# A two-block token mixer on one core: first norm on token rows, kept differences, low-rank products among the gate units

## The reference

```
h  = x * rsqrt(mean(x*x over channels) + 1e-6) * a_norm
xx = shift_one_token(h) - h
xr, xw, xk, xv, xa, xg = (h + xx * mu[j] for j in 0..5)
g = xg @ w_in[3]                          # 2048 columns, gate
w_log uses tanh(xw @ w1) @ w2             # w1: 1024 x 64
a     uses (xa @ a1) @ a2                 # a1: 1024 x 64
r, k, v = xr @ w_in[0], xk @ w_in[1], xv @ w_in[2]
... 32-head recurrence over 512 tokens gives y ...
x = x + y @ w_out
```

## Time and profile before

| | |
|---|---|
| median of 3 runs | 2349.39 us (2346.32 to 2353.45) |
| the profiled execution | 2350.47 us, span 2348.7 us |
| PE busy | 2116.7 us (90%), 16706 instructions |
| DVE busy | 1412.9 us (60%) |
| ACT busy | 1005.9 us (43%) |
| POOL busy | 266.6 us (11%) |
| DMA | 217.50 MB, mean 93 GB/s |

### The profile page before, as it was taken

One profiled execution on the slowest core, in us unless ns is written; L12 is line 12 of the kernel. 1 busy time (PEld: TensorE's weight loads), 2 busy tenths in 40 slices (PEclk: granted clock), 3 DMA queues, 4 the chain that ended last, 5 costly groups with the idle time before them and its releaser, 6 DMA issues.

```text
span 2348.7 us, 43326 instructions
## 1 busy us (share of the span) xinstructions
PE 2116.7 (90%) x16706; PEld 1653.7 (70%) x16706; DVE 1412.9 (60%) x2214; ACT 1005.9 (43%) x1768; POOL 266.6 (11%) x233
## 2 busy tenths in 40 slices
PE   2799999988888886989999999887989998999998
PEld 1577777767777774868888888566756675787876
DVE  6777777776676663355544555589755556434345
ACT  3464555545666664132322323321577324323233
POOL 2102000000233223000000000098000000000000
PEclk6899999989999997999999999899999998999998
DMA  3244555572324311323333333122211131333332
GB/s 107 63 129 143 166 168 169 167 180 59 76 68 95 93 30 61 96 73 96 90 103 91 89 97 99 48 78 63 82 45 37 53 90 54 97 91 91 101 90 76
DMA packets 396700, 217.50 MB, mean 93 GB/s; under 512 B 86144, under 2 KB 375320, under 8 KB 396312
## 3 DMA queue, kind: packets, MB, share of 16 engines
q1 hardware_dynamic: 395936, 215.40, 31.6%
q10 hardware_dynamic: 632, 0.21, 0.0%
HBM read 181.94 MB, written 33.62 MB: 92 GB/s over the span
## 4 chain that ended last, share of the span: by engine, by line
PE 67%; DVE 17%; ACT 8%; issue 5%; DMA 1%; SPq 1%; POOL 0%; DVEq 0%; ACTq 0%
PE bank L1502 17%; PE bank L1504 16%; PE bank L1503 16%; PE bank L520 3%; DVE dconv L1915 3%; DVE w_lo L1656 3%; PE bank L497 1%; ACT w_hi L1266 1%; PE bank L528 1%; DVE tmp L1705 1%; PE bank L443 1%; PE bank L429 1%; PE bank L471 1%; PE bank L874 1%; PE bank L865 1%
## 5 line engine op out<-in xcount | busy, mean ns | idle before, releaser
L1502 PE MATMUL bank<-xl,w_hi 128*128 128x512 f32 (+1 forms) x1696 | 689.1, 406 | 58.2 <-DVE xl L1661 40.6
L1503 PE MATMUL bank<-xl,w_lo 128*128 128x512 f32 (+1 forms) x1696 | 667.4, 393 | 0.0
L1504 PE MATMUL bank<-xl,w_hi 128*128 128x512 f32 (+1 forms) x1696 | 666.8, 393 | 0.0
L1266 ACT ACTIVATE w_hi<-w_raw 128x1024 fp32r<-128x1024 f32 (+1 forms) x282 | 295.6, 1049 | 426.3 <-PE bank L1504 421.7
L1502 PEld LDWEIGHTS bank<-xl,w_hi 128*128 128x128 f32 (+1 forms) x1696 | 321.1, 189 | 170.6 <-issue 53.5
L1656 DVE TENSOR_TENSOR w_lo<-w_raw,w_hi 128x1024 fp32r<-128x1024 f32 (+1 forms) x282 | 347.1, 1231 | 123.1 <-ACT w_hi L1266 112.1
L1503 PEld LDWEIGHTS bank<-xl,w_lo 128*128 128x128 f32 (+1 forms) x1696 | 322.1, 190 | 70.3 <-issue 7.4
L1504 PEld LDWEIGHTS bank<-xl,w_hi 128*128 128x128 f32 (+1 forms) x1696 | 321.5, 190 | 69.8 <-issue 1.6
L1502 PE MATMUL bank<-xh,w_hi 128*128 128x512 f32 x480 | 197.9, 412 | 50.3 <-DVE w_lo L1656 45.3
L1503 PE MATMUL bank<-xh,w_lo 128*128 128x512 f32 x480 | 191.9, 400 | 0.0
L1504 PE MATMUL bank<-xh,w_hi 128*128 128x512 f32 x480 | 191.3, 399 | 0.0
(11 more groups left out here) (310 smaller groups left out, 3070.5 us busy)
## 6 DMA issues: line engine op xcount, KB each, us to landing
w_raw<-in_a_w_in SPq DMA_DIRECT2D x64, 512.0 KB, 3.9
w_raw<-in_b_w_in SPq DMA_DIRECT2D x64, 512.0 KB, 4.0
w_raw<-in_w_ffn_up SPq DMA_DIRECT2D x44, 512.0 KB, 3.7
w_raw<-in_w_in SPq DMA_DIRECT2D x36, 512.0 KB, 3.7
w_raw<-in_a_w_out SPq DMA_DIRECT2D x16, 512.0 KB, 3.6
w_raw<-in_b_w_out SPq DMA_DIRECT2D x16, 512.0 KB, 3.7
w_raw<-in_w_ffn_down SPq DMA_DIRECT2D x16, 512.0 KB, 3.6
d_g<-sq SPq DMA_DIRECT2D x16, 256.0 KB, 2.1
```

The source lines that it names most:

```text
L1266: A(w_hi[0:rows, slot, 0:nkb, 0:ncol], w_raw[0:rows, slot, 0:nkb, 0:ncol], ACT.Copy).then_inc(s_hi, 1)
L1502: mm(outp, wh, xlo, start=start, stop=False)
L1503: mm(outp, wl, xhi, start=False, stop=False)
L1504: return mm(outp, wh, xhi, start=False, stop=stop)
```

## The change

What it does, part by part:

- x is loaded as four row blocks (128 tokens each) into `x_raw`. ACT squares a block with a sum along the row (`accum_out`) and makes the reciprocal root as one number a token; DVE scales the block in place; PE turns it. The eight banks hold the turned tiles, and ACT writes `hT` from them, with `a_norm` as the scale of the copy. `xT`, the eight squares, their sums and the PE sum go.
- The token differences are kept in `xx` (8 tiles, in the place of `xT`): tile 0 by DVE, tiles 1 to 7 by POOL. `shift_difference` in the gate turns goes.
- Units 0 and 1 (low-rank) go; the first unit is gate unit 0. The low-rank first products are made from h and xx instead of xw and xa: `xw @ w1 = h @ w1 + xx @ (mu * w1)`. POOL scales w1 and a1 by mu; their copies are split once by ACT and DVE. In each of the first four gate turns ACT makes the high parts of two tiles of h and two of xx (`lora_input`), POOL the low parts, and PE adds 12 matmuls into bank 6 behind the odd unit (`first_lora`). The hidden layer's steps follow in turns 4 to 7, and its last step stands behind turn 7.
- Parameters: one group is loaded by ACT's queue at first, the other three by SP's behind the first panels; they are turned behind unit 0 and copied behind turn 0.
- The store of `xT` and its load go. x is loaded a second time as rows (`x_back`) behind the last loads of the recurrence, PE turns it in the last turn of the recurrence's loop (`x_back_turned`), DVE copies it to `xT2` before it splits Y.

The core of the diff:

```diff
-U_LORA1 = 0
-U_GATE = U_LORA1 + 2
+U_GATE = 0
...
+            def x_back_turned(k):
+                if k == 0:
+                    pe.wait_ge(s_back, 16)
+                if k >= 4:
+                    pe.wait_ge(s_xt, k - 3)
+                for q in range(NT):
+                    last = tr(bank[k % 4][:, q * P:(q + 1) * P], x_back[:, q, k * P:(k + 1) * P], ident[:])
+                last.then_inc(s_xtr, 1)
...
+                    if t == PAIRS + 1 and s < DK:
+                        x_back_turned(s)
...
+            sp.dma_start(x_back[:], i["x"].rearrange("b (q p) d -> p (b q) d", p=P)).then_inc(s_back, 16)
             sp.wait_ge(R["y_finished"], CI)
-            sp.dma_start(xT2[:], d_x).then_inc(s_back, 16)
...
-            sp.wait_ge(s_xt, DK)
-            sp.dma_start(d_x, xT[:]).then_inc(s_spill, 16)
-            for u in range(4):
-                gate(u // 2, u % 2)
+            for q in range(NT):
+                sp.dma_start(x_raw[:, q, :], i["x"][0, q * P:(q + 1) * P, :]).then_inc(s_xin[q], 16)
+            gate(0, 0)
+            for n, mat in enumerate((i["a_w1"][0], i["a_a1"][0])):
+                sp.dma_start(w1_raw[:, 0, :, n * LORA:(n + 1) * LORA],
+                             mat.rearrange("(k p) c -> p k c", p=P)).then_inc(s_w1, 16)
+            gate(0, 1)
+            load_params(sp, range(1, 4), s_par[1])
+            for u in range(2):
+                gate(1, u)
...
+            for n, mu in enumerate((1, 4)):
+                gt.tensor_tensor(w1_raw[:, 1, :, cols], w1_raw[:, 0, :, cols], scale, ALU.mult).then_inc(s_w1m, 1)
+            for k in range(1, DK):
+                gp.wait_ge(s_hT, k + 1)
+                gt.tensor_tensor(xx[:, k, :], hT[:, k, 0:T], hT[:, k, 1:T + 1], ALU.subtract).then_inc(s_xx, 1)
+            for t in range(LORA_TURNS):
+                for n in range(4):
+                    gp.wait_ge(s_inhi, 4 * t + n + 1)
+                    gt.tensor_tensor(l_lo[:, n // 2, n % 2, :], ..., l_hi[...], ALU.subtract).then_inc(s_inlo, 1)
...
+            for q in range(NT):
+                act.wait_ge(s_xin[q], 16)
+                A(sq[:]..., x_raw[:, q, :], ACT.Square, accum_out=row_sum[:, q:q + 1]).then_inc(s_sq, 2)
+                act.wait_ge(s_sq, 2 * (q + 1))
+                o(A(r, row_sum[:, q:q + 1], ACT.Ln, bias=eps[:, 0:1], scale=1.0 / D))
+                A(r, r, ACT.Exp, scale=-0.5).then_inc(s_rs, 1)
+            w_high(0, 0, panels_by(0))
...
+            for k in range(DK + 2):
+                if k < DK:
+                    act.wait_ge(s_tr, k + 1)
+                    A(hT[:, k, 1:T + 1], bank[k][:], ACT.Copy, scale=col("a_norm", k)).then_inc(s_hT, 1)
+                if k >= 2:
+                    x_high(X_G + k - 2, xh[:, 0, k - 2, :], k % 2)
+                if k == DK - 1:
+                    act.wait_ge(s_w1, 32)
+                    first_weights(0)
+            first_weights(1)
...
+            for t in range(LORA_TURNS):
+                gate(t)
+                if t + 1 < LORA_TURNS:
+                    lora_input(t + 1)
+            act.wait_ge(s_lora, LORA_TURNS)
+            gate(LORA_TURNS)
+            act.wait_ge(s_lmax, 1)
+            z = acc[rows2[0], :]
+            o(A(z, z, ACT.Exp, scale=-2.0))
+            o(A(z, z, ACT.Ln, bias=1.0))
+            A(z, z, ACT.Exp, scale=-1.0).then_inc(s_lsig, 1)
...
+            def first_lora(t):
+                pe.wait_ge(s_inlo, 4 * (t + 1))
+                for n in range(4):
+                    last = three(bank[6][:], w1_hi[:, n % 2, 2 * t + n // 2, :], w1_lo[...], l_hi[...], l_lo[...], ...)
+                last.then_inc(s_lora, 1)
...
+            for q in range(NT):
+                dve.wait_ge(s_rs, q + 1)
+                V.tensor_scalar(x_raw[:, q, :], x_raw[:, q, :], row_rstd[:, q:q + 1], None, ALU.mult).then_inc(s_sqa, 2)
+            w_low(0, 0)
...
-                    if u == 0:
-                        shift_difference(t)
...
+            dve.wait_ge(s_lhi, 1)
+            V.tensor_tensor(lora[:, 1, :], acc[:], lora[:, 0, :].bitcast(F32), ALU.subtract).then_inc(s_lt, 1)
...
+            dve.wait_ge(R["y_summed"], CI)
+            for k in range(DK):
+                dve.wait_ge(s_xtr, k + 1)
+                if k == DK - 2:
+                    dve.wait_ge(R["y_finished"], CI - 1)
+                V.tensor_copy(xT2[:, k, :], bank[k % 4][:]).then_inc(s_xt, 1)
```

More of the change, by code:

```diff
@@ L1005, in later_panels, with load_params @@
             sp.wait_ge(s_out, 16 * DK // 2)
+        def load_params(eng, groups, loaded):
+            for t in groups:
+                row = 0
+                for name, n in PARAMS[t]:
+                    src = i[name]
+                    letters = " ".join("abcd"[:len(src.shape)])
+                    flat = src.rearrange(f"{letters} -> ({letters})") if len(src.shape) > 1 else src
+                    eng.dma_start(par_raw[row:row + n, t, :], flat.rearrange("(r c) -> r c", c=P)).then_inc(loaded, 16)
+                    row += n
         @block.sync
@@ L1014, in panel @@
                 sp.dma_start(w_raw[0:rows, slot, kb0:kb0 + nkb, at_col:at_col + ncol], src).then_inc(s_raw[slot], 16)
-            sp.dma_start(x_raw[:], i["x"].rearrange("b (q p) d -> p (b q) d", p=P)).then_inc(s_xin, 16)
-            panel(0, 0, i["a_w1"][0], 0, KB, 0, LORA)
-            panel(1, 1, i["a_w1"][0], 0, KB, 0, LORA)
-            panel(1, 1, i["a_a1"][0], 0, KB, 0, LORA, first=False, at_col=LORA)
             def gate(t, u):
@@ L1277, in sigmoid, with norm @@
                 return A(z, z, ACT.Exp, scale=-1.0)
-            def norm(n, x=xT, ready=None):
+            def norm(n, x, ready=None):
                 for k in range(DK if x is not None else 0):
@@ L1298, in _ @@
-            act.wait_ge(s_xt, DK)
-            norm(0)
-            w_high(0, 0, panels_by(0), LORA)
-            w_high(1, 1, panels_by(1))
-            for k in range(DK):
-                x_high(2 * k, xl[0][:, 0, k, :], 0)
-                x_high(2 * k + 1, xl[1][:, 0, k, :], 1)
-            for k in range(DK):
-                x_high(X_G + k, xh[:, 0, k, :], k % 2)
-            act.wait_ge(s_free[0], 1)
-            z = rstd[0:LORA, 0, :]
-            o(A(z, z, ACT.Exp, scale=-2.0))
-            o(A(z, z, ACT.Ln, bias=1.0))
@@ L1555, in phase, with gate_turn @@
                 repeat(pe, turns - 1, turn)
-            phase(U_GATE, 2, CI // 2, xh, X_G)
+            def first_lora(t):
+                pe.wait_ge(s_inlo, 4 * (t + 1))
+                if t == 0:
+                    pe.wait_ge(s_w1lo, 2)
+                    pe.wait_ge(s_hT, 7)
+                for n in range(4):
+                    last = three(bank[6][:], w1_hi[:, n % 2, 2 * t + n // 2, :], w1_lo[:, n % 2, 2 * t + n // 2, :],
+                                 l_hi[:, n // 2, n % 2, :], l_lo[:, n // 2, n % 2, :], t == 0 and n == 0,
+                                 t == LORA_TURNS - 1 and n == 3)
+                last.then_inc(s_lora, 1)
+            for t in range(LORA_TURNS):
+                for u in range(2):
+                    if t == 0:
+                        pe.wait_ge(s_hT, u + 1)
+                    unit(2 * t + u, u, xh, xcount=None if t or u else lambda k: X_G + k + 1, free=t)
+                    if t == 0 and u == 0:
+                        pe.wait_ge(s_par[1], 16 * sum(len(rows) for rows in PARAMS[1:]))
+                        pe.wait_ge(s_hT, 3)
+                        for g in range(1, 4):
+                            last = turn_params(g, 2)
+                        last.then_inc(s_part, 1)
+                first_lora(t)
+            def gate_turn(t):
+                for u in range(2):
+                    unit(2 * t + (2 * LORA_TURNS + u), u, xh, free=t + LORA_TURNS)
+            repeat(pe, CI // 2 - LORA_TURNS, gate_turn)
             def mix(t, a):
@@ L1661, in x_low, with norm @@
                 V.tensor_tensor(lo, tmp[:, buf, :], hi.bitcast(F32), ALU.subtract).then_inc(s_xlo, 1)
[L1663 removed]
+            def norm(n, gain, dst, x, summed=False):
                 for k in range(0 if summed or n in SUMMED_BY_PE else DK):
@@ L1735, in gate, with last_params @@
+            def last_params():
+                dve.wait_ge(s_part, 2)
+                for t in range(1, 4):
+                    o(V.tensor_copy(par[:, t, 0:PAR_ROWS[t]], bank[2][:, t * P:t * P + PAR_ROWS[t]]))
+                t_ka, r_ka = PAR_AT["a_ka"]
+                o(V.tensor_scalar(neg_ka[:], par[:, t_ka, r_ka:r_ka + CI], -1.0, 1.0, ALU.mult, ALU.add))
             def gate(t):
```

233 lines of the change are left out of this document (124 added, 109 removed).

## The result

The changed kernel takes **2316.64 us** (median of 4 runs, 2313.35 to 2317.88), the kernel before beside it 2351.42 (4 runs): ratio 0.9853, 95% interval 0.9838 to 0.9868, so 34.8 us faster. Forecast were 2302 with a range of 2293 to 2315: the direction is right, the time is 14.6 us over the forecast and 1.6 over the range. The profiled execution took 2317.88 (span 2316.2).

What follows compares the result with a forecast made beforehand. TensorE holds 67% of the chain, so the gain must come from its idle time, mostly before the first mixing unit. Start -54, gate turns +8.1, reload -1 make -47 from 2349.4: 2302 us, range 2293 to 2315.

Steps and rivals of the forecast that it cites:

- Matmul work hardly changes: Whole kernel: 48 low-rank matmuls go and 48 return, at 0.23 us each; the gain must come from TensorE's idle time.
- Start: Up to the even unit of turn 1: reached at 44 us against 98.05, a change of -54 us.
- The 2.05 a tile: Start, unit 0: VectorE and GpSimd together pace the tiles at 2.05 us while differences are still made.
- the four products' 2.75: End of the start, behind unit 1: the first four low-rank products add 12 matmuls of 0.23, 2.75 us.
- ends near 41.7 and is covered: End of the start: VectorE's way to the next even panel ends near 41.7 us, hidden behind TensorE's work.
- Gate turns: From the even unit of turn 1 to the first mixing unit: 98.2 us against 90.1, a change of +8.1.
- They can hold DVE steps by 0.6, mostly within the 1.8 of slack: First low-rank gate turns: GpSimd's four low parts can delay VectorE by 0.6 us, mostly absorbed by 1.8 of slack.
- Difference costed at nothing: Gate turns: removing VectorE's 0.68 us difference gains nothing because ACT is as late as before; upper bound 7 us.
- Reload: Second load of x near 930 us: the DMA wait goes, transposes add some delay; -1.0 us, range -2.5 to +0.5.
- A: Start and gate turns: helper engines become the bound, 2.7 us a tile and slower low-rank turns; 2313 us, chance 0.22.
- B: Start at 1.36 us a tile, unit 1 at full clock, removed difference gains 0.3 a turn; 2294 us, chance 0.17.
- C: Gate turns: TensorE stays at its lower clock, 0.41 us a matmul instead of 0.23; 2380 us, chance 0.02.

Runs made afterwards that it cites:

- p4: The changed kernel, unchanged, run and profiled again on the same chip as the layout runs; 2318.90 us, ratio 0.9841 to the kernel before.
- p3: The changed kernel with row_sum and row_rstd laid over w2_raw, so activation tiles keep the addresses of the kernel before; 2313.61 us.
- e1: Against p3: parameters turned after the first row block, two row blocks scaled ahead of the parameter copy, tile 7 turned last; 2312.39 us.
- e6: Against p3: in turn 1 alone, GpSimd's low parts wait for VectorE's low part of the odd panel; 2309.41 us.
- e2: Against p3: in turns 0 to 3, GpSimd's low parts wait for VectorE's low parts of the low-rank weights or odd panel; 2314.80 us.
- e7: Against p3: the old kernel's difference subtraction put back on VectorE in gate turns 0 to 3, result unused; 2313.35 us.
- e3: The kernel before with the new reload of x alone; 2352.35 us against 2355.44.
- e5: Against e1: GpSimd makes the token differences of tiles 1 to 7 ahead of scaling the low-rank weights; 2308.62 us.
- e8: Against p3: edits of e5 and e6, and TensorE's first mixing unit no longer waits for inputs it doesn't read; 2308.39 us.
- b1: Against e8: the third mixing panel's load issued ahead of the store of the last odd gate on SyncE's queue; 2303.31 us.

## Why the prediction was off

**The sum assumed that unchanged matmuls keep their pace; that is the step that failed most.** "Matmul work hardly changes" priced each at 0.23 us, before and after. The count stayed, the step went from 227.0 to 228.9 ns, through the distance between the weight and the activation tiles: +7.3 us in the profiled stages, 5.3 us in the medians of p4 and p3. The two new lines of `place` stood in the full diff and the prediction went past them. With that term taken out (p3, 2313.61) the time lies inside the range, still 11.6 over the forecast; against the kernel before beside it (2355.84) it wins 42.2 us of the 47 told.

**Start, -54 forecast, -50.5 measured.** The square's 1.04 and the one-column steps were right (1.06 and 0.29, 0.20, with 0.19 more to read the row sum: 1.6 a block, ACT done at 11.14). The first hT was to follow at 13.0 and came at 15.96, because VectorE's scaling stood behind the parameter copy at 9.27, a queue that the prediction did not walk, and the 32 transposes, told to need 0.17 each and not to hold ACT, took 6.36 us behind it. e1 confirms the place, and that 1.2 of its 2.8 us arrive. The 2.05 a tile was right, unit 0 ended at 36.4 and not 32, of which 3 came from here. Unit 1 ran at full clock in 5.7 us where 7.8 was taken, which gave 2.1 back, and it ended at 42.6, 1.3 late. The other 2.2 us of the 3.5 came behind it, where the prediction saw only the four products' 2.75: they waited for GpSimd's low parts, which took 7.8 us beside VectorE and not 5.5, and the even unit waited for VectorE's panel.

```profile
43.85 0.50 PE L1584 MATMUL bank<-l_lo,w_hi 128*128 128x512 f32 x1 [1.25 <-POOL l_lo L1261]
...
46.26 1.22 DVE L1766 TENSOR_TENSOR w_lo<-w_raw,w_hi 128x1024 fp32r<-128x1024 f32 x1
47.39 0.68 DVE L1838 TENSOR_SCALAR rstd<-bank 128x512 f32<-128x512 f32 x1
47.53 0.51 PE L1584 MATMUL bank<-xh,w_hi 128*128 128x512 f32 x1 [0.66 <-DVE w_lo L1766]
```

Of VectorE's way to that panel the prediction said that it "ends near 41.7 and is covered"; it was ready at 47.47, 5.8 later. Some 3.2 of these it began late, 2.2 are the low-rank weight parts beside GpSimd (4.54 against 2.35).

**Gate turns, +8.1 forecast, +11.8 measured.** Turns 1 to 7 were told as 14.4, 14.1, 13.75, 12.3, 13.8, 12.4 and 17.4 and took 18.31, 13.70, 15.06, 12.10, 13.34, 12.21 and 17.21. Five of seven are within 0.5; turns 1 and 3 miss by 3.9 and 1.3. "They can hold DVE steps by 0.6, mostly within the 1.8 of slack" is the sentence that failed. A GpSimd subtraction beside a panel's low part costs VectorE 0.9 to 1.0 (2.12 and 2.22 against 1.22), and in turn 1 the slack wasn't there: the previous odd unit's clamp, laid out 1.8 us ahead of the even unit, stood behind the even panel in VectorE's queue and came 0.14 ahead (47.39). That made a pause of 2.58 us where 0.3 was told; without GpSimd in the way 1.74 of it remained (e6). Behind it the odd unit of turn 1 ran 7.4 us, in part at clock 0.50, instead of 5.8. Neither was in the 14.4. e2 shows GpSimd's part of it, and also that delaying GpSimd only moves the wait.

**Difference costed at nothing**: nearly right in the steady turns. From clamp to the end of the next even panel's low part it is 6.42 before and 6.27 after, and turns 4 and 6 take 12.10 and 12.21 where a turn before took 12.33: 0.1 to 0.2 a turn. In turn 0 it would have cost 0.6 (e7).

**Reload, -1.0 forecast, -3.6 measured**, outside the -2.5 to +0.5. Both upsides were named, the 1.7 at the panel (1.8 measured) and the warmer TensorE (0.93 a pair on two pairs, 1.85 measured); the transposes were feared as work in the way, and with them among the pairs the granted clock stayed at 1.00. No norm sum is later for them in e3.

**Rivals.** A (the helpers bound, 2313) comes nearest in time, and in part in cause: turn 1 was bound by VectorE and GpSimd, but the tiles kept to 2.1, and 7 of the 14 us are another matter. B is refuted in its tiles at 1.36 and in its gain of 0.3 a turn; its unit 1 at full clock came true, at 2.1 us. C (the clock stays low) happened behind the start once, in part of one unit.

## What to carry to other kernels

When a diff adds or moves a tile ahead of large ones, work out the new distance between the tiles that one matmul reads, and count matmuls in a stretch where TensorE is never idle, in both traces, before explaining a drift by anything else. When an engine's first steps are costed, walk its queue in order: what stood in front here (the parameter copy, the weight scaling, a store on SP's queue) was each time short and unrelated. A cure for one wait should be run on the chip, since of the seven edits here that took one away (e1, e2, e3, e5, e6, e8, b1) only e3 and b1 kept their gain whole. And before a slowed instruction is called slow, look at what ended just before it: in the overlaps of VectorE and GpSimd the record held a wait.
